# Block inverses of a head pair: the backward direction moved to the other two quarters of the array, transposed, in seven levels

## What is computed

```python
def step(state, inp):                      # for every token, per head, in each direction
    r_t, w_t, k_t, v_t, a_t, b_t = inp     # a = -kk, b = kk * a
    sa = jnp.einsum('bhvk,bhk->bhv', state, a_t)
    state = state * w_t[:, :, None, :] + sa[..., None] * b_t[:, :, None, :] + v_t[..., None] * k_t[:, :, None, :]
    return state, jnp.einsum('bhvk,bhk->bhv', state, r_t)
```

## Time and profile before

| | us |
|---|---|
| median of 3 runs | 2027.83 |
| lowest, highest | 2014.14, 2028.31 |
| the profiled execution | 2029.15 |
| its span, first to last instruction | 2027.2 |
| layer 0, GLA stage and two-pair stage begin | 477.9, 601.4 |
| layer 1, GLA stage and two-pair stage begin | 1459.1, 1579.1 |

### The profile page before, as it was taken

How to read it: one execution, slowest core, us unless ns; L and a number is a source line. 1 busy time by engine, 2 the same in 40 slices (tenths; PEclk the granted TensorE clock), 3 DMA queues, 4 the chain that set the end, 5 groups by cost and what they waited for, 6 DMA issues and landing times. The chain is left out here.

```text
span 2027.2 us, 38671 instructions
## 1 busy us (share of the span) xinstructions
PE 1910.2 (94%) x16360; PEld 1748.5 (86%) x16360; DVE 1095.8 (54%) x1845; ACT 739.1 (36%) x1108; POOL 33.2 (2%) x62
## 2 busy tenths in 40 slices
PE   5999999998888989999999999999978898999997
PEld 2888999995665879999999999999747497999997
DVE  3544444865537466554455554476564756655533
ACT  3333333435224244333343333344441424433322
POOL 0000000000001000000000000000000100000000
PEclk9999999998789999999999999999979798999999
DMA  7766233423446233333343333442240401333332
GB/s 271 263 224 222 90 129 137 158 101 113 142 129 212 85 109 125 124 124 113 127 145 124 124 118 114 138 169 90 87 148 4 159 13 66 125 124 124 105 128 89
DMA packets 73192, 263.25 MB, mean 130 GB/s; under 512 B 9696, under 2 KB 10848, under 8 KB 56928
## 3 DMA queue, kind: packets, MB, share of 16 engines
q1 hardware_dynamic: 73056, 261.27, 37.9%
HBM read 259.08 MB, written 2.16 MB: 129 GB/s over the span
## 5 line engine op out<-in xcount | busy, mean ns | idle before, releaser
L157 PE MATMUL ps<-h_head,w_head 128*128 128x386 f32 x1824 | 624.0, 342 | 9.2 <-DVEq L243 4.1
L157 PE MATMUL ps<-h_head,w_rest 128*128 128x386 f32 x1824 | 619.3, 340 | 0.0
L157 PE MATMUL ps<-h_rest,w_head 128*128 128x386 f32 x1824 | 617.3, 338 | 0.0
L219 ACT ACTIVATE w_head<-w_raw 128x2048 fp32r<-128x2048 f32 (+1 forms) x176 | 303.0, 1721 | 609.2 <-PE ps L157 598.9
L222 DVE TENSOR_TENSOR w_rest<-w_raw,w_head 128x2048 fp32r<-128x2048 f32 (+1 forms) x176 | 360.7, 2049 | 204.4 <-ACT w_head L219 204.3
L157 PEld LDWEIGHTS ps<-h_head,w_head 128*128 128x128 f32 x1824 | 345.9, 190 | 28.6 <-issue 18.8
L157 PEld LDWEIGHTS ps<-h_head,w_rest 128*128 128x128 f32 x1824 | 345.8, 190 | 0.0
L157 PEld LDWEIGHTS ps<-h_rest,w_head 128*128 128x128 f32 x1824 | 343.0, 188 | 0.2
L157 PE MATMUL ps<-gu_head,w_head 128*128 128x384 f32 x832 | 279.9, 336 | 11.4 <-DVE gu_rest L813 11.4
L157 PE MATMUL ps<-gu_rest,w_head 128*128 128x384 f32 x832 | 279.4, 336 | 0.0
L157 PE MATMUL ps<-gu_head,w_rest 128*128 128x384 f32 x832 | 279.3, 336 | 0.0
(11 more groups left out here) (294 smaller groups left out, 1798.1 us busy)
## 6 DMA issues: line engine op xcount, KB each, us to landing
w_raw<-in_w_in SPq DMA_DIRECT2D x88, 1024.0 KB, 4.8
w_raw<-in_w_out SPq DMA_DIRECT2D x64, 704.0 KB, 4.0
w_raw<-in_ada_w SPq DMA_DIRECT2D x41, 1024.0 KB, 6.2
ada_raw<-in_ada_w SPq DMA_DIRECT2D x31, 1024.0 KB, 6.4
w_raw<-in_mix_in SPq DMA_DIRECT2D x26, 1024.0 KB, 4.9
w_raw<-in_mix_out SPq DMA_DIRECT2D x8, 1024.0 KB, 5.0
hyena_const<-in_hconst SPq DMA_DIRECT2D x2, 1792.0 KB, 9.6
x<-in_x_in SPq DMA_DIRECT2D x1, 1536.0 KB, 12.2
```

The lines of the kernel that those rows point to most:

```text
L157: return nc.tensor.matmul(out, lhsT, rhs, start=start, stop=stop)
L219: return nc.scalar.activation(self.HI[src], self.RAW[src], ACT.Copy)
```

## The change

The inverse is rewritten. Direction 0 stays on the diagonal quarters; direction 1 reads partitions `half(h)` and writes `half(1 - h)`, the two other quarters, into a second bank. A product turned into its other half comes out for the transposed problem, and the series is regrouped so that factors (1 + power) multiply T: with d4, t1, x4, t2, x8, t, q, ex, g, y1, ex2, y behind level 1. Steps called `crossed` issue 24 products over four quarters, both directions at once; the two `straight` steps (t, y) issue 24 on the diagonal quarters alone. Copies now take both directions, two banks, in one instruction (`both`). There are seven levels behind one another instead of nine.

Each pair has four banks of its own: `A` 0 to 3, GLA 4 to 6, `B` 4 to 7. Bank 7 is also adaLN's, so `B` waits for the first set's bias, and the second set of adaLN products waits for `B`'s y1.

The orders are rewritten. In the two-pair stage `B` and `A` are prepared in step, all twelve gram groups stand ahead of the first level, the inverses and the state loops of both alternate, and the second set of adaLN units stands behind the inverse. In the GLA stage four units of set 1 (before: three) stand ahead of level 1, four more between the levels, none in the state loop; the second unit of set 0 stands ahead of the gate norm; GLA's norm stands ahead of the first state step.

```diff
-            def each(self, b, lhsT, rhs):
-                for c, e in PROBS:
-                    last = mm(bank(b, TOK)[half(e), c * C:c * C + C], lhsT(c, e), rhs(c, e))
+            def crossed(self, ba, bb, lhsT, rhs):
+                for c in range(NCH):
+                    for h in range(2):
+                        mm(bank(ba, TOK)[half(h), c * C:c * C + C], lhsT[half(h), 0, c, :], rhs[half(h), 0, c, :])
+                    for h in range(2):
+                        last = mm(bank(bb, TOK)[half(1 - h), c * C:c * C + C], lhsT[half(h), 1, c, :], rhs[half(h), 1, c, :])
+                return last
+            def straight(self, ba, bb, lhsT, rhs):
+                for z, b in enumerate((ba, bb)):
+                    for c in range(NCH):
+                        for h in range(2):
+                            last = mm(bank(b, TOK)[half(h), c * C:c * C + C], lhsT[half(h), z, c, :], rhs[half(h), z, c, :])
...
+            def pe_d4(self, pe):
+                self.after_act(pe, "d2_1")
+                self.after_dve(pe, "x2_1")
+                self.pe_step(self.crossed(*self.even(), self.X, self.D2), "d4")
+            def pe_t1(self, pe):
+                self.after_dve(pe, "j2_1")
+                self.after_pool(pe, "q1")
+                self.pe_step(self.crossed(*self.odd(), self.J2, self.T), "t1")
...
+            def dve_one_plus(self, dve, product, out, banks, name):
+                self.after_pe(dve, product)
+                ones = cst("istack").unsqueeze(1).unsqueeze(1).to_broadcast([128, 2, NCH, C])
+                self.tt(out, self.both(banks), ones, ALU.add, name)
...
-                A = Pair(scope, SEMS[0:5], lay, 1, (0, 1, 2), 6, PR, TG, AL, MO)
-                B = Pair(scope, SEMS[5:10], lay, 2, (3, 4, 5), 6, PR, TG, AL, MO, (A.act_done, A.AC["s6_1"]))
+                A = Pair(scope, SEMS[0:5], lay, 1, (0, 1, 2), 3, PR, TG, AL, MO)
+                B = Pair(scope, SEMS[5:10], lay, 2, (4, 5, 6), 7, PR, TG, AL, MO, (SEMS[16], 1))
...
                         if s and kt == 0:
                             pe.wait_ge(bias_done, s)
+                            pe.wait_ge(B.act_done, B.AC["y1"])
```

The order of PE in the new two-pair stage, from the gram groups on:

```diff
+                    B.pe_gram(pe, 1, 2)
+                    A.pe_gram(pe, 1, 2)
+                    B.pe_s1(pe, 0)
+                    A.pe_s1(pe, 0)
+                    A.pe_s1(pe, 1)
+                    B.pe_s1(pe, 1)
+                    A.pe_d4(pe)
+                    A.pe_t1(pe)
+                    B.pe_d4(pe)
+                    A.pe_x4(pe)
+                    B.pe_t1(pe)
+                    B.pe_x4(pe)
+                    A.pe_t2(pe)
+                    A.pe_x8(pe)
+                    B.pe_t2(pe)
+                    B.pe_x8(pe)
+                    A.pe_t(pe)
+                    B.pe_t(pe)
+                    A.pe_q(pe)
+                    A.pe_ex(pe)
+                    B.pe_q(pe)
+                    B.pe_ex(pe)
+                    A.pe_g(pe)
+                    B.pe_g(pe)
+                    A.pe_y1(pe)
+                    A.pe_ex2(pe)
+                    B.pe_y1(pe)
+                    B.pe_ex2(pe)
+                    A.pe_y(pe)
+                    ada_products(pe, 1, 0)
+                    B.pe_y(pe)
+                    A.pe_x(pe, 0)
```

More of the change, by code:

```diff
@@ L1513, in pe_s1 @@
                     pe.wait_ge(*self.shared_free)
[L1514 to L1530, removed]
@@ new lines, in pe_s1 @@
+                for b, lhsT, rhs in ((ba, self.X, self.D), (bb, self.D, self.X)):
+                    for c in range(NCH):
+                        for h in range(2):
+                            last = mm(bank(b, TOK)[half(h), c * C:c * C + C], lhsT[half(h), z, c, :], rhs[half(h), z, c, :])
+                self.pe_step(last, f"s1_{z}")
+            def pe_d4(self, pe):
+                self.after_act(pe, "d2_1")
+                self.after_dve(pe, "x2_1")
+                self.pe_step(self.crossed(*self.even(), self.X, self.D2), "d4")
@@ new lines, in pe_x8, with pe_t, pe_q @@
+            def pe_x8(self, pe):
+                self.after_dve(pe, "x4")
+                self.pe_step(self.crossed(*self.even(), self.D4, self.X4), "x8")
+            def pe_t(self, pe):
+                self.after_dve(pe, "j8")
+                self.pe_step(self.straight(*self.odd(), self.J8, self.T), "t")
+            def pe_q(self, pe):
+                self.after_act(pe, "t_0")
+                self.after_dve(pe, "t_1")
+                for c in range(NCH):
+                    for h in range(2):
+                        mm(bank(self.b0, TOK)[half(h), c * C:c * C + C], self.INV[half(h), 0, c, :], cst("istack", 0, None, 64 * h, 64 * h + 64))
+                    for h in range(2):
+                        last = mm(bank(self.b1, TOK)[half(1 - h), c * C:c * C + C], self.INV[half(h), 1, c, :],
+                                  cst("istack", 0, None, 64 * h, 64 * h + 64))
+                self.pe_step(last, "q")
@@ L1566, in pe_x, with pe_ex2, pe_y @@
+            def pe_ex2(self, pe):
+                self.after_act(pe, "gm")
+                self.after_dve(pe, "ex")
+                self.pe_step(self.crossed(*self.even(), self.G, self.EX), "ex2")
+            def pe_y(self, pe):
+                self.after_dve(pe, "jg")
+                self.after_act(pe, "y1")
+                self.pe_step(self.straight(*self.even(), self.JG, self.Y1), "y")
             def pe_x(self, pe, t):
                 if t == 0:
-                    self.after_dve(pe, "s9_1")
+                    self.after_dve(pe, "y_0")
+                    self.after_act(pe, "y_1")
@@ new lines, in dve_t, with dve_one_plus_ex, dve_ex, dve_one_plus_ex2 @@
+            def dve_t(self, dve):
+                self.after_pe(dve, "t")
+                self.dve_step(nc.vector.tensor_copy(self.INV[:, 1, :, :], self.one_of(self.odd(), 1)), "t_1")
+            def dve_one_plus_ex(self, dve):
+                self.dve_one_plus(dve, "ex", self.JE, self.odd(), "je")
+            def dve_ex(self, dve):
+                self.after_pe(dve, "ex")
+                self.dve_step(nc.vector.tensor_copy(self.EX, self.both(self.odd())), "ex")
+            def dve_one_plus_ex2(self, dve):
+                self.dve_one_plus(dve, "ex2", self.JG, self.even(), "jg")
```

592 lines of the change are left out of this document (270 added, 322 removed).

## The result

The changed kernel takes 2050.7 us (median; 2047.0 to 2058.0), the kernel before 2023.6 us beside it. The ratio is 1.0137, with a 95% interval of 1.0112 to 1.0161: 28 us slower, where 14 us faster was forecast, and outside the range that ended at 2036. The profiled execution of the changed kernel is 2057.99 us, its span 2056.2, 29 us over that of before.

What follows compares the result with a forecast made beforehand. It took TensorE's queue as the bound in the two-pair inverse; gains of 2.7 + 2.0 + 4.9 + 4.7 = 14.3 us off 2029.15 gave 2014.9, as a median 2014 us. Likeliest 2007 to 2022, range 2000 to 2036.

Steps and rivals of the forecast that it cites:

- The unit: Inverse on TensorE: twelve 64x64 products take 0.70 us, and a crossed step of 24 was taken at 0.70 too.
- crossed steps queue: Rival, inverse: second pair of quarters queues behind the first, 1.40 us a crossed step, 2045 us in all; chance 0.12.
- rule on weight loads: Skill's rule: weight loads overlap running products only when the row group differs, so a crossed step would cost 1.40 us.
- The sum over the array's time alone: Inverse on TensorE: 18 units for 26 before, 12.6 us for 18.2 a pair, 33.6 us less for six pairs.
- If a crossed step costs one unit: Inverse: ten crossed steps at 0.70 us each, giving 4 + 10 + 4 = 18 units a pair.
- first rival: The rival that crossed steps queue at 1.40 us each: 30.6 us on top, 2045 us; chance 0.12.
- The chain and the gram rounds: Two-pair stage, layer 1: level 1 starts 6.6 us later, then 50.5 us to the mean for 62.2; gain 4.9.
- nothing is given back: Rival, two-pair stages: gram rounds delay level 1 by 2 us, not 6.6; 2004 us; chance 0.22 for 2004 or below.
- GLA stage: GLA stages: gain of 2.7 us in layer 1, where x0 starts at 25.9 after level 1, and 2.0 in layer 0.
- I take nothing: GLA stage's start: adaLN unit moved ahead of the gate norm costs nothing, or 1.3 us a stage if not covered.
- Clock: Rival: TensorE's granted clock falls in gram rounds and inverse, 2033 us; chance 0.18, shared with unseen waits, for 2022 to 2035.
- The sign that was named: Sign against the forecast: a wait of several us on ScalarE or POOL, which it priced at nothing.

Runs made afterwards that it cites:

- wide: Changed kernel with each crossed step and the inverse's turn as 12 products of 128 moving columns instead of 24 of 64, halving instructions: 2019.2 us, ratio 0.9977.
- gla_only: Kernel before with the changed inverse, order and bank layout in the two GLA stages alone: 2033.6 us, ratio 1.0044.
- split: Changed kernel with each product of the nine crossed steps (not the turn) made as two of 32 moving columns: 2120.4 us, ratio 1.0466.
- gla_only_front: gla_only with the second adaLN unit put back behind the second decay group, not ahead of the gate norm: 2027.3 us, ratio 0.9998.
- apart: Changed kernel with each crossed step issuing its twelve diagonal-quarter products first, the other twelve behind them, same instructions: 2056.3 us, ratio 1.0151.

## Why the prediction was wrong, step by step

- **The unit** held where instructions had come in. Crossed steps start 0.70 us apart, and the earlier trace rows had been the right rows to read. The rival "crossed steps queue" fell as a mechanism: the quarters overlap. By the rule on weight loads that the prediction cites beside it a step would have cost 1.40; the trace decides against that.
- **The sum over the array's time alone was the step that failed.** It counted 10 units instead of 20 for ten steps, and never the instructions in them: 1344 for a pair now, 1152 before. At 70 in a us these are 19.2 and 16.5 us. "If a crossed step costs one unit" took a step at 0.70 us; with its instructions it costs 1.37. The array's 12.6 us is no longer the bound; the pair's work on TensorE is worth 19.2 against the old 18.2. The warning stood in the earlier trace rows: x24 product records in 0.70 us and as many weight loads, 69 instructions in a us; the densest row shown, x144 in 3.01 us, has 96 and lasts 3 us. I took the lack of idle time in 38 us as TensorE being bound by its array, and never asked what a plain group left to spare; it was 2%.
- **The rival's price came true by another way.** 96 instructions at 70 in a us are 1.37 us a crossed step, next to the 1.40 of the first rival, and its 2045 us was the nearest number of the text. It had 0.12.
- **The chain and the gram rounds** held where instructions come in time. In layer 1's two-pair stage level 1 started at +51.1 us (forecast +52.3), 5.5 us later than before for 6.6. From there to the mean 61.5 us less 10.8 of issue waits are 50.7; forecast 50.5, and `wide` has 50.3, with steps that are a little shorter. That the numbers agree within 0.2 us is in part luck, as each step was priced from rows of other groups. The two-pair stages of `wide` are 4.8 and 5.8 us shorter than before; the forecast was 4.7 and 4.9. Six gram rounds took 13.0 us for 12.8. Their start is less well founded: the numbers beside it give 1618.0 (1621.04 less five passes of 0.6) and not 1617.2. The bet that the gram rounds would cost less (0.22 for "nothing is given back") was lost.
- **GLA stage.** x0 came 27.7 us after level 1 for 27.7 before and a forecast of 25.9, x1 34.5 for 35.5 and 32.9; 1.4 us of it are issue waits. Where instructions come in time the gain is there: `wide` takes 48.9 us from level 1 to the mean for 51.9 (forecast 2.7 less), and in layer 0 50.5 without its issue wait for 52.6 (forecast 2.0 less). What was mis-sized is the front, "I take nothing": 10 us in all, by the ring of loads. The sentence that a later wait for weights covers the moved unit had the sign wrong: the later wait grows, because the moved unit delays the use that frees the slot of the load waited for.
- **Clock.** The rival fell: the granted clock was 0.96 (layer 0) and 1.00 (layer 1) in the two-pair inverse, and in layer 1 0.83 ahead of it for 0.80 before.
- **The sign that was named** ("a wait of several us ... which I price at nothing") was the right thing to look for, on the wrong engines.

In the sum of the prediction's terms: 29 us for late instructions (`wide` less its wider products), 10 for the front, 14.3 forecast gained: -14.3 + 29 + 10 = +25 us, measured +28. The 29 are an estimate (26 to 29), and the 10 were measured in the kernel before and in `gla_only`; in the changed kernel itself putting the line back gave no clear gain.

## What to carry to other kernels

Before making TensorE's work denser, count its instructions and not only its array time: product records plus weight loads in a us, against what the trace shows to come in over several packets (here about 70). A short group can be denser, as the one of 3 us at 96 was. If the new pace is above it, halving the array time buys nothing; fewer and wider products do. And a unit of work that frees a load's slot should be placed by the load that waits for it, not by the idle time it fills.

## What the runs showed of the hardware that was not expected

- Where TensorE starved, its instructions came in packets of 16 KB, one in 3.7 us (3.4 to 4.2 from wait to wait, with 254 instructions), about 70 in a us, in the changed kernel as in `split`, there at full clock and at half.
- Little is kept ahead: one or two packets, by 750 instructions from the start of level 1 to the first wait with two packets on their way.
- A packet came later while other DMAs filled the engines: waits of 3.1 and 3.9 us in the changed kernel behind windows at a DMA share of 1.01 and 0.93, and up to 4.2 us in `gla_only_front`; at most 2.0 us with the engines idle. One of 2.8 us (layer 0's two-pair stage) began when the loads had just ended.
- Four quarters of 64x64 worked at once, 24 products in 0.70 us. Two groups on different quarters overlapped even when one was issued behind the other: 1.06 us a step in `apart` for 2 x 0.70.
- Six products of 128 columns took 0.655 us, twelve of 64 columns 0.70.
